# Two-block transformer on one Trainium2 core: attention heads between the levels of the inverse, part of the output projection in the solve

## The reference, cut to what matters

```python
def sb(q, k, v):                      # strictly causal, 8 heads of 64
    z = q @ k.T / 8
    log_rest = where(s < t, log_sigmoid(-z), 0)
    suffix = cumsum_from_the_right(log_rest) - log_rest
    return where(s < t, exp(log_sigmoid(z) + suffix), 0) @ v   # then an RMS norm per head

def step(state, r, w, k, v, kk, a):   # RWKV-7, kk normed per head
    sa = state @ -kk
    state = state * w + outer(sa, kk * a) + outer(v, k)
    return state, state @ r           # then a group norm per head, a bonus and a gate

h = h + concat([o_sb, o_rw]) @ w_out  # then a router and 32 experts, then block two
```

## Time and profile before

| | us |
|---|---|
| median of 3 runs | 1950.2 |
| lowest and highest | 1947.29, 1950.61 |
| the profiled execution | 1945.84 |
| its span, first to last instruction | 1944.1 |
| preparation on PE (99.0 to 165.1) | 66.1 |
| inverse from unit 4 on (165.1 to 227.3) | 62.2 |
| solve (227.3 to 272.0) | 44.7 |
| `dev` and `w_out` (272.0 to 303.3) | 31.3 |

### The profile page before, as it was taken

The page is one execution under the profiler, slowest core; times in us unless marked ns, Lnnn a source line. Parts: engine busy times, 40 slices in busy tenths (PEclk is TensorE's granted clock), DMA queues, the critical chain, the costliest instruction groups (busy, mean ns, idle before and its releaser), DMA issues.

```text
span 1944.1 us, 26397 instructions
## 1 busy us (share of the span) xinstructions
PE 1865.8 (96%) x10950; PEld 1618.1 (83%) x10950; DVE 1199.4 (62%) x1500; ACT 951.1 (49%) x1241; POOL 97.8 (5%) x82
## 2 busy tenths in 40 slices
PE   7979998999999999998999999999999999999999
PEld 7968977788888878888979788888887898888887
DVE  5435437867777775545976665546554696766553
ACT  5562215646555464435655454435443566436442
POOL 1004202100000000000020000000000011000000
PEclk9989979999999999999999999999999999999999
DMA  8400004689999935553513356555655360246553
GB/s 277 165 4 1 1 22 163 217 304 335 337 337 343 317 126 177 192 188 115 175 43 109 124 180 187 181 194 178 190 183 174 115 195 28 90 149 193 176 194 108
DMA packets 191064, 329.95 MB, mean 170 GB/s; under 512 B 7776, under 2 KB 150496, under 8 KB 186592
## 3 DMA queue, kind: packets, MB, share of 16 engines
q1 hardware_dynamic: 190800, 327.74, 51.1%
q0 software_dynamic: 144, 0.52, 0.1%
HBM read 327.18 MB, written 1.05 MB: 169 GB/s over the span
## 4 chain that ended last, share of the span: by engine, by line
PE 79%; DVE 13%; ACT 4%; DMA 2%; issue 1%; SPq 0%; POOL 0%; DVEq 0%; ACTq 0%; POOLq 0%
PE ps L524 77%; DVE rlo L1386 3%; PE ps L527 2%; DVE arena L1375 2%; ACT rhi L2135 2%; ACT arena L2135 1%; DMA ring<-in_exp_w_up 1%; DMA ring<-in_w_in 1%; DVE arena L1378 1%; DVE xnl L1375 1%; ACT L2135 1%; DVE arena L1984 1%; DVE small L2043 0%; DVE xtok L1375 0%; DVE small L1930 0%
## 5 line engine op out<-in xcount | busy, mean ns | idle before, releaser
L1386 DVE TENSOR_TENSOR rlo<-ring,rhi 128x2048 fp32r<-128x2048 f32 x274 | 628.4, 2295 | 372.4 <-ACT rhi L2135 371.9
L2135 ACT ACTIVATE rhi<-ring 128x2048 fp32r<-128x2048 f32 x274 | 521.4, 1906 | 283.6 <-PE ps L524 139.1
L524 PE MATMUL ps<-rhi,xnh 128*128 128x512 f32 (+1 forms) x768 | 301.3, 392 | 0.0
L524 PE MATMUL ps<-rhi,xnl 128*128 128x512 f32 (+1 forms) x768 | 296.4, 386 | 0.0
L524 PE MATMUL ps<-rlo,xnh 128*128 128x512 f32 (+1 forms) x768 | 296.0, 385 | 0.0
L524 PE MATMUL ps<-xnh,rhi 128*128 128x256 f32 (+2 forms) x824 | 240.0, 291 | 4.3 <-DVE xnl L1375 2.8
L524 PE MATMUL ps<-xnl,rhi 128*128 128x256 f32 (+2 forms) x824 | 234.4, 285 | 0.0
L524 PE MATMUL ps<-xnh,rlo 128*128 128x256 f32 (+2 forms) x824 | 234.2, 284 | 0.0
L524 PE MATMUL ps<-arena 128*128 128x128 f32 (+8 forms) x1448 | 209.7, 301 | 18.3 <-DVE arena L2050 9.4
L524 PEld LDWEIGHTS ps<-arena 128*128 128x128 f32 (+3 forms) x1448 | 173.1, 182 | 43.5 <-issue 11.1
L524 PE MATMUL ps<-rhi,hhi 128*128 128x512 f32 x544 | 204.9, 394 | 0.0
(11 more groups left out here) (226 smaller groups left out, 2194.0 us busy)
## 6 DMA issues: line engine op xcount, KB each, us to landing
ring<-in_w_in SPq DMA_DIRECT2D x47, 1024.0 KB, 5.4
ring<-in_ffn_w_gate SPq DMA_DIRECT2D x88, 512.0 KB, 4.0
ring<-in_ffn_w_up SPq DMA_DIRECT2D x88, 512.0 KB, 5.0
ring<-in_ffn_w_down SPq DMA_DIRECT2D x44, 1024.0 KB, 4.9
ring<-in_exp_w_down SPq DMA_DIRECT2D x35, 1024.0 KB, 5.7
ring<-in_exp_w_gate SPq DMA_DIRECT2D x66, 512.0 KB, 4.3
ring<-in_exp_w_up SPq DMA_DIRECT2D x66, 512.0 KB, 5.4
ring<-in_w_out SPq DMA_DIRECT2D x20, 1024.0 KB, 4.9
```

The source lines that it names most:

```text
L524: return e.matmul(o, lhsT, rhs, start=start, stop=stop, skip_group_check=True)
L1386: e.tensor_tensor(lo, raw, f32(hi), SUB).then_inc(*w.hit("lo", n))
L2135: return e.activation(o, x, func, **kw)
```

## The change

What it does, by part:

1. `kk`'s head norm moves ahead: DVE computes `kk0` before the first split, ACT squares it before `sb_proj(0)`'s eviction, PE does `head_sums` before `sb_proj(1)` and `head_spread` before `sb_proj(2)`. DVE does `km` between `head_sums` and `head_rec`, and makes its splits one at a time between these steps. EN, EP on ACT move behind `sb_proj(1)`.
2. The mask of a head's scores is one matmul in the split format on copies (`ident_s`, `mneg_s`) instead of two in float32.
3. Only the scores of heads 0 to 3 stand before the inverse. Then `at`, the token rows, level 0 (now 16 transposes) and the bonus follow. Everything else of the heads is put between the levels of the inverse: `sb_weights`, `sb_scores` (4 to 7) and `sb_values` on PE, their ACT and DVE steps likewise.
4. The inverse computes only XT by matmul and gets X by 4 transposes (`level_turn`), which ACT copies out; Y is copied out by DVE instead of ACT. The last level works on the 64x64 corner. All units share banks 0, 1 and 2.
5. The attention's own head norm stands around `masked(0)`; `w_out` row 0 is cut in four parts of 3 matmuls put into the solve, with sums in banks 0, 1, 2 and 7. The second split by `ahead(ld("w_out", 0))` moves behind the solve on ACT and DVE. The turned tiles of the norm use banks 3 to 6.

```diff
-                mm(PS[b][:, 0:128], C("ident"), C("mnegs"), False, False)
-                mm(PS[b][:, 256:384], C("ident"), C("mnegs"), False, True).then_inc(*w.hit("sb_z", h))
+                w.wait_ge("sb_mask")
+                mm(PS[b][:, :].rearrange("p (a t) -> p a t", a=4)[:, 0:4:2], ident_s, mneg_s[:, None, :].to_broadcast([128, 2, 128]),
+                   False, True).then_inc(*w.hit("sb_z", h))
...
+                w.wait_ge("m", u)
+                bank(u % 2, ("x0", u))
+                for i in range(4):
+                    p = tr(PS[u % 2][:, i * 128:i * 128 + 128], M[:, u % 3, i])
+                p.then_inc(*w.hit("ly", u))
+
+            def level_y(u):
+                li, g = units[u]
+                w.wait_ge("m", u)
+                w.wait_ge(*(("x0", g) if li == 1 else ("xa", li - 1, g)))
+                bank(0, ("y", u))
+                for i in range(4):
+                    if li < LAST:
+                        p = mm(PS[0][:, i * 128:i * 128 + 128], M[:, u % 3, i], X[:, 4 * g + i], True, True)
+                    else:
+                        p = mm(PS[0][64:128, i * 128:i * 128 + 64], M[0:64, u % 3, i, 64:128], X[0:64, 4 * g + i, 0:64], True, True)
+                p.then_inc(*w.hit("ly", u))
+
+            def level_x(u):
+                li, g = units[u]
+                w.wait_ge("y", u)
+                w.wait_ge("x", li - 1, g)
+                bank(1, ("x", li, g))
+                for i in range(4):
+                    if li < LAST:
+                        p = mm(PS[1][:, i * 128:i * 128 + 128], Y[:, 4 * g + i], XT[:, 4 * g + i], True, True)
+                    else:
+                        p = mm(PS[1][0:64, i * 128:i * 128 + 64], Y[64:128, 4 * g + i, 0:64], XT[64:128, 4 * g + i, 64:128], True, True)
+                p.then_inc(*w.hit("lx", u))
+
+            def level_turn(u):
+                li, g = units[u]
+                w.wait_ge("x", li, g)
+                bank(2, ("xa", li, g))
+                for i in range(4):
+                    p = tr(PS[2][:, i * 128:i * 128 + 128], XT[:, 4 * g + i])
+                p.then_inc(*w.hit("lt", u))
...
+                for u in range(4, NU + 2):
                     if u < NU:
                         level_y(u)
-                    if u and units[u - 1][0]:
+                    if 6 <= u < 10:
+                        sb_weights(u - 6)
+                    if 10 <= u < 14:
+                        sb_scores(u - 6)
+                    if 11 <= u < 15:
+                        sb_values(u - 11)
+                    if 19 <= u < 23:
+                        sb_weights(u - 15)
+                    if 23 <= u < 27:
+                        sb_values(u - 19)
+                    if 4 <= u - 1 < NU:
                         level_x(u - 1)
+                    if 4 <= u - 2 < NU and units[u - 2][0] < LAST:
+                        level_turn(u - 2)
...
+                else:
+                    w_out_part(0, 1)
...
+            def w_out_part(k, b):
                 n = take(ld("w_out", k // 2))
                 wh, wl_ = parts(n)
-                for tt in range(2):
-                    for dh in range(2):
-                        d = slice(512 * dh, 512 * dh + 512)
-                        p = mm3(PS[4 + 2 * tt + dh][:, :], xnh[:, k, tok(tt)], xnl[:, k, tok(tt)], wh[:, k % 2, d], wl_[:, k % 2, d], k == 0, False)
-                if k % 2:
+                if k == 0:
+                    w.wait_ge("sb_lo")
+                    bank(sum_bank("w_out", b), ("sum", "w_out", b))
+                tt, d = b // 2, slice(512 * (b % 2), 512 * (b % 2) + 512)
+                p = mm3(PS[sum_bank("w_out", b)][:, :], xnh[:, k, tok(tt)], xnl[:, k, tok(tt)], wh[:, k % 2, d], wl_[:, k % 2, d], k == 0, False)
+                if k % 2 and b == 3:
                     p.then_inc(*w.hit("w_out", k // 2))
                     spent[n] = ("w_out", k // 2)
+
...
+                w.wait_ge("kk_sq")
+                head_sums(sqk, 2, "kk")
                 sb_proj(1)
+                head_spread((3, 1), "kk", (("kk", 0), ("kk", 1)))
...
+                for h in range(4):
+                    sb_scores(h)
+                w.wait_ge("zT", 1)
+                w.wait_ge("bT", 1)
...
                     for i in range(4):
                         p = mm(PS[g][:, i * 128:i * 128 + 128], bT[po:po + 64, i, s], zT[po:po + 64, i, s], True, True)
                     p.then_inc(*w.hit("at_mm", g))
-                sb_step(7)
+                token_rows(2, um[:, 8:12], tok(0), 0)
+                token_rows(3, um[:, 8:12], tok(1), 1)
+                level_first(0)
...
+                token_rows(2, bT, tok(0), 2)
+                token_rows(3, kT, tok(0), 3)
+                level_first(2)
+                level_first(3)
+                for half in range(2):
+                    w.wait_ge("bonus", 3)
+                    bank(2 + half, ("bon", half))
+                    mm(PS[2 + half][:, :], C("bones"), bonus_[:, 2 * half:2 * half + 2], True, True).then_inc(*w.hit("bon_mm", half))
                 inverse()
+                w.wait_ge("sb_sq")
+                head_sums(sq2, 4, "sb")
                 masked(0)
+                head_spread((5, 6), "sb", (("sb_m", 1), ("sb_m", 3)))
                 solve(0)
                 outputs(0)
                 solve(1)
                 state()
                 outputs(1)
                 solve(2)
+                w_out_part(0, 0)
                 outputs(2)
...
                 solve(3)
+                w_out_part(0, 2)
                 outputs(3)
+                w_out_part(0, 3)
...
+                w_out_row(1)
                 w.wait_ge("dev_sq")
-                head_sums(sqd, 2, "gn")
-                w_out_row(1)
-                head_spread((3, 0), "gn", (("gn", 0), ("gn", 1)))
+                head_sums(sqd, 5, "gn")
                 w_out_row(2)
+                head_spread((6, 4), "gn", (("gn", 0), ("gn", 1)))
                 w_out_row(3)
```

DVE and ACT, the parts that the prediction speaks of:

```diff
+                for f in range(4):
+                    w.wait_ge("um", 4 + f)
+                    p = ts(kkT[:, f], um[:, 4 + f], pr("k_k", f), None, MUL)
+                p.then_inc(*w.hit("kk0"))
                 w.dma(d_later, 80)
-                for i in range(4):
-                    ahead(ld("sb", i))
+                e.tensor_copy(ident_s, C("ident"))
+                e.tensor_copy(mneg_s, C("mnegs")).then_inc(*w.hit("sb_mask"))
+                ahead(ld("sb", 0))
                 e.memset(Cc[:, :, 0:1], 0.0)
...
-                ahead(ld("sb", 4))
+                ahead(ld("sb", 1))
...
                 head_sums(2, 1e-24, None, MAX, None, "kk")
-                sb_step(1)
-                head_rec("kk")
-                for i, b in enumerate((3, 1)):
-                    w.wait_ge("hr_spread", "kk", i)
-                    e.tensor_tensor(kkT[:, 2 * i:2 * i + 2], kkT[:, 2 * i:2 * i + 2], two(b), MUL).then_inc(*w.hit("kk", i))
-                sb_step(2)
                 w.wait_ge("a", 1)
+                w.wait_ge("kk0")
                 for f in range(4):
                     own(ts(tmp[2][:, f], aT[:, f], 1.0, pr("k_a", f), SUB, MUL))
                     p = stt(um[:, 4 + f], tmp[2][:, f], 1.0, um[:, 4 + f], ADD, MUL)
                 p.then_inc(*w.hit("km"))
-                sb_step(3)
+                head_rec("kk")
+                ahead(ld("sb", 2))
+                for i, b in enumerate((3, 1)):
+                    w.wait_ge("hr_spread", "kk", i)
+                    e.tensor_tensor(kkT[:, 2 * i:2 * i + 2], kkT[:, 2 * i:2 * i + 2], two(b), MUL).then_inc(*w.hit("kk", i))
                 w.wait_ge("kk", 1)
                 own(e.tensor_tensor(aT, aT, kkT, MUL))
+                ahead(ld("sb", 3))
...
+                ahead(ld("sb", 4))
                 w.wait_ge("rk")
                 for f in range(4):
-                    ts(tmp[0][:, f], tmp[0][:, f], pr("r_k", f), None, MUL).then_inc(*w.hit("bonus", f))
+                    ts(bonus_[:, f], bonus_[:, f], pr("r_k", f), None, MUL).then_inc(*w.hit("bonus", f))
...
                 inverse()
+                head_sums(4, 1.0 / 64, 1e-6, MUL, ADD, "sb")
                 masked(0)
+                head_rec("sb")
+                for f in range(4):
+                    w.wait_ge("hr_spread", "sb", f // 2)
+                    stt(sbo[:, f], sbo[:, f], pr("sb_out_g", f), PS[5 + f // 2][:, 256 * (f % 2):256 * (f % 2) + 256], MUL, MUL).then_inc(*w.hit("sb_m", f))
                 masked(1)
+                w.wait_ge("sb_hi")
+                e.tensor_tensor(xnl[:, 0:4], sbo, f32(xnh[:, 0:4]), SUB).then_inc(*w.hit("sb_lo"))
...
+                ahead(ld("w_out", 0))
+                head_sums(5, 1.0 / 64, 64e-5, MUL, ADD, "gn")
...
+                w.wait_ge("kk0")
+                act(sqk, kkT, ACT.Square).then_inc(*w.hit("kk_sq"))
...
+                ahead(ld("sb", 1))
+                head_sqrt("kk")
                 sb_proj(1)
+                w.wait_ge("decay", 0)
+                w.wait_ge("decay", 1)
```

(10 more changed lines are left out.)

299 lines of the change are left out of this document (116 added, 183 removed).

## The result

| | us |
|---|---|
| before, median of 20 runs | 1951.07 (1943.93 to 1957.87) |
| after, median of 20 runs | 1933.58 (1925.15 to 1954.95) |
| ratio, with its 95% interval | 0.9912 (0.9892 to 0.9932) |
| profiled execution, before and after | 1945.84, 1934.19 |

Four executions are slow ones at a low clock (1955 here, 2647 of e1, 1970 of e10, 2320 of e13), and the ratios and the medians of the experiments leave them out; the changed kernel's median is 1933.1 without its own.

A forecast was written before the change was run, and what follows sets the result against it. PE, busy 96% of the span, was taken as the bound. Terms 7.3 - 48.8 + 10.0 + 3.7 - 2.3 - 5.0 = -35.1 took 1945.84 to 1910.7; with 4.4 for the median, 1915 us, range 1902 to 1933.

The forecast's parts named there:

- term 1: Ahead of the scores: kk's norm moved ahead adds a longer ACT wait, head_sums, a reciprocal wait and head_spread, +7.3 us.
- term 3: The inverse: cheaper units, but heads' work put into it and stalls; 62.2 to 72.2 us, +10.0.
- term 2: The preparation, scores to unit 4: shrinks from 66.1 to 17.3 us, -48.8, with 3.0 added for half clock.
- Term 6: Solve and w_out: full-size w_out parts bring back half of the 10.1 us lost to half clock, -5.0 us.
- term 4: The solve: head_spread, its wait and the four w_out parts added, less 2.1 us of covered waits, +3.7 us.
- rival (a): The clock falls in the inverse: 1970 us with 55 us at half clock; chance 0.08.
- Rival (b): The inverse's units become a chain, each of 24 growing by 0.7 us for DVE's uncovered copy: 1932 us; chance 0.14.
- Term 5: Behind the solve: w_out row 0 is gone, 2.7 us, less 0.4 for down_tiles reaching unsplit weights: -2.3 us.
- Rival (c): The experts swallow the gain if their weights come no sooner: 1950 us; chance 0.03.

The follow-up runs named there:

- e1: The changed kernel with the four w_out parts taken out of the solve, row 0 whole behind the dev matmuls: 1937.0 us.
- e10: The changed kernel with eight idle 512-column matmuls, only where PE waits in the solve: 1930.2 us.
- e13: e11 plus ten more idle 512-column matmuls around the last level of the inverse: 1917.7 us.
- e5: The changed kernel with DVE's two multiplications of kk by the reciprocal norm ahead of the split ahead(ld('sb', 2)): 1927.9 us.
- e6: The changed kernel with kk's head norm one projection later and DVE's kk multiplications ahead of its next split: 1927.7 us.
- e7: The changed kernel with the scores of heads 0 to 3 spread between the last projections and at, not in one piece: 1928.8 us.
- e12: The changed kernel with e6 and e7 joined, plus the attention's head norm behind masked(0), without idle matmuls: 1920.7 us.
- e9: The changed kernel with the attention's head norm later: head_sums behind masked(0), head_spread behind solve(0): 1939.1 us.
- e15: e11 with its twenty idle matmuls replaced, in the same places, by twenty of 64 columns in float32: 1934.3 us.
- e11: The changed kernel with e6 and e7 joined, plus twenty idle 512-column matmuls in the solve: 1920.0 us.
- e4: The changed kernel with the last level of the inverse on whole 128x128 matrices instead of the 64x64 corner: 1930.7 us.
- e8: The changed kernel with DVE's two bonus multiplications behind the copy of Y of unit 5 instead of ahead of unit 4's: 1930.0 us.
- e3: The changed kernel with forty idle 128x128 transposes in the solve, two for each idle matmul of e2: 1931.3 us.
- e2: The changed kernel with twenty idle 512-column matmuls added in the solve: 1930.8 us.

## Why the prediction was wrong

Faster was right, the size was not: the profile gained 11.7 us where the sum said 35.1. Of the missing 23.4 us some 9.6 lie in the solve, 4.6 in term 1, 2.9 in term 3, 0.7 in term 2, and 5.8 outside the terms (1.3 ahead of `lw`, 4.5 behind the experts' start).

- **Term 6, the clock in the solve, is the step that failed.** It took full-size `w_out` parts to bring back half of the loss, 3.8 us in the solve. Instead the half clock from `masked(0)` to `dev` went from 15 us to 27, which costs 5.8 us more. Without the clock the stage grew by 9.5 - 5.8 = 3.7, just as term 4 said. The four parts of 0.7 us stand at 238.75, 247.62, 249.82 and 258.02, behind 33 us of narrow matmuls. The first ran at half clock itself, and at 248.6 the clock fell again, right behind the second: parts of this size did not hold it. The ends given for this term, -10.1 and 0, had none above zero, though the change puts `head_sums` and `head_spread`, both narrow, beside the stage. Why this execution lost more than the one of before is open: executions of this same solve lost between 11 and 38 us, and there is one of before.
- **Term 1, +7.3, was +11.9.** The wait for ACT grew by 0.9, `head_sums` took 2.1, `head_spread` 1.9. The wait of 2.5 for the reciprocal did not come, because `sb_proj(1)` ran at half clock from 71 to 78 and took 8.6 us instead of 5.8: 2.8 in its place. That is 7.7, close to the 7.3. What the prediction missed is DVE's order: the split behind `head_rec` waited 7.17 us for ACT, whose `EN`, `EP` and their table load stood first, and `g`'s bank came free only behind it: 2.17 us of wait, and 3.5 of half clock behind that cost 1.7. e5 and e6 show it.
- **Term 2, -48.8, was -48.1.** Its 3.0 for half clock was 6.8/2 = 3.4 measured. e7 shows it can be avoided.
- **Term 3, +10.0, was +12.9.** The units are at the pace of the count, 2.2 us for 2.3. The eight `sb_values` take 0.8 us each, 6.4 where 5.0 was counted from a row without its end. Stalls were taken at 1.2 and are 2.5, all ahead of unit 5, where DVE's level-0 adds and the bonus stand before its copy; the waits of the last level are 0.8 for 1.0. And `head_sums` ran partly at half clock, 2.3 for 1.8. The clock is 1.00 up to `head_sums`, so rival (a) did not come, and transposes in a fifth of each unit did not make the clock fall.
- **Rival (b)** gave 1932, close to the 1933.6 measured, and that is chance: the units follow one another every 2.2 us, and from unit 6 to the last level PE waits nowhere.
- **Term 5, -2.3, with the clock in `w_out`,** came out at -3.6 for -3.5.
- **Rival (c)** had a chance of 0.03 and 4.5 us of the profile look like it. From the experts' start to the end it takes 1559.4 us before and 1563.9 after, but in the other kernels (e10 left out), whose experts start between 351.7 and 387.0, 1559.8 to 1566.5 without order. The experts wait for DMA (ACT 123 us in total for weights in the changed kernel, 118 before), and that is spread between executions; the profiled one of before has the least of all. It isn't shown that the earlier start costs anything.

At its upper end the range let the clock give back nothing in the solve; it didn't let it lose more. As an estimate: with the solve at half clock nearly throughout, as in e1's profile, 40 us more of it cost 20, so 1934 + 20 = 1954, and the runs of the changed kernel reach 1952.

## What to carry to other kernels

Where a stage is made of small matmuls, count its clock as open on both sides, from almost none to all of it at half, and look at the spread of the runs and the mean clock of each before believing one profile. Moving narrow steps between wide ones gave 3.7 us in the profile (e7), and moving kk's norm 7.1 (e6); together, in e12 (with the later norm, which by itself gave nothing in e9), they are 12 us in the medians without any added work. Filling a narrow stage with idle wide matmuls was not shown to beat that; idle narrow ones lost all of it. When a step is put ahead of another engine's split, follow that engine's list to the next operation for which PE's bank waits.

## What the runs showed of the hardware

- The granted clock stays at one half for tens of us while PE is busy: 68.9 of 72.9 us in e1's profile, at a mean of 0.53, with no wait above 0.94. The Trainium skill ("TensorE: Matmul & The Clock Gate", on oscillation) puts such falls down to PE standing idle; here PE hardly stood idle. With the waits filled by narrow work (e15) 47 us ran at half clock, by wide work (e11) 10.6.
- The same program loses different amounts in the same stage. The solve had 11, 28, 31, 31, 38 and 38 us at half clock in profiles of kernels whose solve is the same (e4, after, e6, e8, e5, e7), and the runs of the changed kernel spread by 26.5 us.
- Transposes of 128x128 in a fifth of each unit of the inverse went with a clock of 1.00 over 72.7 us. With forty idle ones in the solve (e3) 14.0 us ran at half clock, with wide matmuls (e2) 10.6, but without either it was 10.7 in e4, so the idle ones show nothing sure.
